# A hybrid decoder step: one Strassen stage for the SSD projections, the gates and the key search, with its weight sums on GpSimd

## The reference

```python
x = x + 0.5 * g1 * swiglu(h, p['w_ffn1_in'], p['w_ffn1_out'])
...
q, k, v, qi, ki, wi, z, xbc, dt_raw, gate_a, gate_s = jnp.split(h @ p['w_in'], split_points(), axis=-1)
...
att = attend(q, k, v, qi, ki, wi)
ssd_y, ssm_new, conv_new = ssd_branch(z, xbc, dt_raw, conv_state, ssm_state, p)
merged = jax.nn.sigmoid(gate_a) * (att @ p['w_attn_out']) + jax.nn.sigmoid(gate_s) * (ssd_y @ p['w_ssd_out'])
x = x + g2 * (merged @ p['w_out'])
...
x = x + 0.5 * g3 * swiglu(h, p['w_ffn2_in'], p['w_ffn2_out'])
```

## Time and profile before

| what | us |
|---|---|
| median of 3 runs (lowest, highest) | 4564.63 (4562.23, 4566.98) |
| the profiled execution | 4567.95 |
| its span | 4566.2 |
| mean granted clock of TensorE | 0.923 |
| the four SSD groups, 1396.31 to 2742.08 | 1345.8 |
| gates and gathers, 2773.7 to 3057.0 | 283.3 |
| attention of the prompt, 3059.8 to 3358.3 | 298.5 |
| second FFN, 3709.0 to 4523.6 | 814.6 |

### The profile page before, as it was taken

One profiled execution on the slowest core, in us unless ns is written; L12 is line 12 of the kernel. 1 busy time (PEld: TensorE's weight loads), 2 busy tenths in 40 slices (PEclk: granted clock), 3 DMA queues, 4 the chain that ended last, 5 costly groups with the idle time before them and its releaser, 6 DMA issues. The chain is left out here.

```text
span 4566.2 us, 47951 instructions
## 1 busy us (share of the span) xinstructions
PE 4077.6 (89%) x17644; PEld 2978.1 (65%) x17644; DVE 2345.6 (51%) x3956; ACT 764.7 (17%) x1512; POOL 292.7 (6%) x325
## 2 busy tenths in 40 slices
PE   6999999969897979979879877988999879999997
PEld 4888888846564646645646644654546558888885
DVE  3444444420038878879789785304453044444444
ACT  2111111121021201201201200015620021111111
POOL 0000000000000200200200200305400000000000
PEclk8999999989968979979979978989998989999999
DMA  4333333241331011011011011220021212222221
GB/s 178 111 138 120 120 122 113 80 195 60 95 56 39 16 55 41 11 57 39 13 55 39 15 53 54 85 93 20 10 70 60 74 55 92 84 81 95 83 86 72
DMA packets 105162, 335.20 MB, mean 73 GB/s; under 512 B 18632, under 2 KB 54736, under 8 KB 86464
## 3 DMA queue, kind: packets, MB, share of 16 engines
q1 hardware_dynamic: 89984, 280.03, 18.2%
q10 hardware_dynamic: 11808, 31.85, 1.9%
q0 software_dynamic: 3200, 21.11, 1.3%
HBM read 289.56 MB, written 43.56 MB: 73 GB/s over the span
## 5 line engine op out<-in xcount | busy, mean ns | idle before, releaser
L737 PE MATMUL banks<-h,arena 128*128 128x344 f32 x1920 | 567.7, 459 | 36.5 <-DMA arena<-in_w_ssd 36.5
L737 PEld LDWEIGHTS banks<-h,arena 128*128 128x128 f32 x1920 | 370.7, 193 | 233.7 <-issue 47.9
L572 ACT ACTIVATE f_u<-f_Y 128x258 f32<-128x258 f32 x408 | 157.7, 387 | 1101.2 <-PE f_Y L510 1101.2
L737 PE MATMUL banks<-y,arena 128*128 128x344 f32 x768 | 239.3, 474 | 38.0 <-DVE y L1938 30.2
L653 DVE TENSOR_TENSOR f_g<-f_u,f_Z 128x258 f32<-128x258 f32 x136 | 57.7, 424 | 390.8 <-PE f_Z L510 390.8
L2122 PE MATMUL gg_ps<-h,gg_w 128*128 128x344 f32 x768 | 234.8, 470 | 9.8 <-DMA gg_w<-in_w_g 9.2
L737 PE MATMUL pja_ps<-h,pja_w 128*128 128x344 f32 x720 | 211.1, 457 | 27.3 <-DMA pja_w<-in_w_att 27.3
L737 PEld LDWEIGHTS banks<-y,arena 128*128 128x128 f32 x768 | 151.7, 199 | 125.6 <-issue 35.7
L2122 PEld LDWEIGHTS gg_ps<-h,gg_w 128*128 128x128 f32 x768 | 151.7, 199 | 90.8 <-DMA gg_w<-in_w_g 10.0
L623 DVE TENSOR_TENSOR f_g<-f_u,f_X 128x258 f32<-128x258 f32 x136 | 57.6, 424 | 292.8 <-PE f_X L510 292.5
L737 PEld LDWEIGHTS pja_ps<-h,pja_w 128*128 128x128 f32 x720 | 138.2, 192 | 100.2 <-issue 29.9
(11 more groups left out here) (354 smaller groups left out, 6814.6 us busy)
## 6 DMA issues: line engine op xcount, KB each, us to landing
raw<-in_w_f1i SPq DMA_DIRECT2D x44, 1024.0 KB, 4.8
raw<-in_w_f2i SPq DMA_DIRECT2D x44, 1024.0 KB, 4.7
f_wa<-in_w_ada SPq DMA_DIRECT2D x14, 2048.0 KB, 9.6
arena<-in_w_ssd SPq DMA_DIRECT2D x40, 512.0 KB, 3.6
raw<-in_w_f1o SPq DMA_DIRECT2D x16, 1024.0 KB, 4.7
raw<-in_w_f2o SPq DMA_DIRECT2D x16, 1024.0 KB, 4.8
n_w<-in_w_ada SPq DMA_DIRECT2D x4, 2048.0 KB, 19.9
scr_kidx<-pja_pages POOLq DMA_DIRECT2D x4, 2048.0 KB, 7.7
```

What stands on the lines that cost most here:

```text
L572: nc.scalar.activation(u[:, i % 2, n], bank[i % 2][:, 0:SUB], ACT.Copy).then_inc(done, 1)
L737: m = nc.tensor.matmul(ps[q][:, c, 0:NC], slots[:, q, k], rhs[:, k, c * NC:(c + 1) * NC], start=k == 0, stop=k == kt - 1)
```

## The change

A new stage, `dense`, stands in place of the four `ssd_project` and of the gates' projection. It runs 28 pairs of output tiles (for each group three convolved ones x, two gate pairs in between, two of z), two halves of columns each, so 56 steps of 7 Strassen products (each 4 matmuls of 128 x 258). `weight_sums` is now told its engine: in `ffn` it is still VectorE, in `dense` GpSimd (`pair_sums`), two pairs ahead. The results go to DRAM: convolved tiles to `scr["xc"]`, activated z and gates to `z`, `gs`, `ga`.

The key search is part of the same stage. The threshold of each row is built bit by bit in 32 steps: `counts` counts on VectorE the scores at or above a candidate (six prompt rows, and the sample scores as two columns of 129 per partition), `vote` adds the sample counts over partitions with one small matmul, and `decide` fixes the bit. Nine later steps mark the chosen keys (`choose`, `choose_samples`).

`index_scores` makes sample scores with four batches side by side in TensorE's column groups (`dot`), a relu and a weighting matmul (`weigh`), and holds four batches of keys at once; they stay in SBUF (`sc2`). `ssd_scan` is written out without a loop and gets its chunks by transfers from DRAM. At the scan's end x and z are loaded for `ssd_post`, which has the skip, gate and norm of `ssd_out` but no projection. `project_and_gather` makes the output projection of all four groups at once, 16 tiles deep, and multiplies it by the gate from DRAM, with a batch's gathers behind each of 8 tiles. `attend` turns up to three chunks ahead and weighs two at a time.

```diff
-def weight_sums(dve, nc, raw, out, made, n):
+def weight_sums(eng, on, raw, out, made, n):
...
+    on.tensor_tensor(s1, a21, a22, ALU.add).then_inc(made, 1)
+    on.tensor_tensor(s3, a11, a21, ALU.subtract).then_inc(made, 1)
+    eng.wait_ge(made, UP + n + 1)
+    on.tensor_tensor(s2, s1, a11, ALU.subtract).then_inc(made, 1)
+    eng.wait_ge(made, UP + n + 3)
+    on.tensor_tensor(s4, a12, s2, ALU.subtract).then_inc(made, 1)
...
-def top_round(dve, nc, rows, m8, found, tick, before):
-
-
-    dve.wait_ge(found, UP + before)
-    dve.sem_inc(tick, 1)
-    for i, s in enumerate(rows):
-        nc.vector.max(m8[0:s.shape[0], i], s).then_inc(found, 1)
-    dve.wait_ge(found, UP + before + len(rows))
-    dve.sem_inc(tick, 1)
-    for i, s in enumerate(rows):
-        nc.vector.match_replace(s, m8[0:s.shape[0], i], s, TAKEN).then_inc(found, 1)
...
+def dense_pairs():
+
+    out = []
+    for g in range(SG):
+        other = [("gs" if g < 2 else "ga", None, (2 * g + n) % 4) for n in range(2)]
+        out += [("x", g, 0), other[0], ("x", g, 1), other[1], ("x", g, 2), ("z", g, 0), ("z", g, 1)]
+    return out
+
...
+            def pair_sums(p):
+                pool.wait_ge(w_in[p % RING], UP + 16 * (p // RING + 1))
+                if p >= SRING:
+                    pool.wait_ge(p3, UP + 2 * (p - SRING) + 2)
+                    pool.wait_ge(p7, UP + 2 * (p - SRING) + 2)
+                weight_sums(pool, nc.gpsimd, raw[:, p % RING].rearrange("p (i k m) -> p i k m", i=4, k=KP), sums[:, p % SRING], made_s, 4 * p)
+
+            for q in range(XB):
+                nc.gpsimd.memset(xb[:, q, :, 0:PAD], 0.0).then_inc(padded, 1)
+            for p in range(SRING):
+                pair_sums(p)
+            for p in range(M):
+                if p in rank:
+                    _, g, j = PAIR[p]
+                    t = g * XT + 2 * j
+                    filled(pool, p)
+                    nc.gpsimd.tensor_copy(raws[:, t:t + 2], xb[:, p % XB, :, PAD + SEQ:PAD + TOK]).then_inc(collected, 1)
+                if p + SRING < M:
+                    pair_sums(p + SRING)
 
...
-            project_tiles(pe, nc, w, ps, h, w_in, mm, read, XT + 4)
+            def product(i, lhs, which, bank, fresh, done):
+                for k in range(KP):
+                    m = nc.tensor.matmul(bank[i % 2][:, 0:SUB], lhs[:, k], column(i, which, k), start=fresh and k == 0,
+                                         stop=k == KP - 1, skip_group_check=not fresh)
+                m.then_inc(done, 1)
+
+            def vote(i):
+                if i < BITS:
+                    pe.wait_ge(counted, UP + (nb + 2) * (i + 1))
+                    if i:
+                        pe.wait_ge(bis, UP + 2 * i)
...
+            for i in range(N + 1):
+                if i < N:
+                    if i % 2 == 0:
+                        pe.wait_ge(w_in[i // 2 % RING], UP + 16 * (i // 2 // RING + 1))
+                    if i >= 2:
+                        pe.wait_ge(yread, UP + i - 1)
+                    product(i, left(i, 0), "11", Y, True, p1)
+                    if i >= 2:
+                        pe.wait_ge(xread, UP + i - 1)
+                    product(i, left(i, 1), "21", X, True, p2)
+                if i >= 1:
+                    pe.wait_ge(u3, UP + i)
+                    product(i - 1, left(i - 1, 3), "t4", Y, False, p4)
+                if i < N:
+                    pe.wait_ge(made_h, UP + 4 * (i % 2 + 1) if i < 2 else UP + 8)
+                    pe.wait_ge(u1, UP + i + 1)
+                    pe.wait_ge(made_s, UP + 4 * (i // 2) + 4)
+                    product(i, total(i)[:, 1], "t2", Y, False, p6)
+                if i >= 1:
+                    pe.wait_ge(zhalf, UP + i)
+                    product(i - 1, total(i - 1)[:, 3], "22", Z, False, p3)
+                if i < N:
+                    if i >= 2:
+                        pe.wait_ge(zread, UP + i - 1)
+                    product(i, total(i)[:, 0], "t1", Z, True, p5)
+                    pe.wait_ge(u2, UP + i + 1)
+                    product(i, total(i)[:, 2], "t3", Y, False, p7)
+                vote(i)
...
+            def counts(j, ns):
+                for n in ns:
+                    scratch, done = (pre, eq)[n % 2], (nb + 2) * j + n
+                    if done >= 2:
+                        dve.wait_ge(counted, UP + done - 1)
+                    src = rows[n] if n < nb else sc2[:, n - nb]
+                    nc.vector.tensor_scalar(scratch[:, 0:src.shape[1]], src, thr(n), None, ALU.is_ge, ALU.add,
+                                            accum_out=count[:, n:n + 1]).then_inc(counted, 1)
+
+            def decide(j):
+                dve.wait_ge(counted, UP + (nb + 2) * (j + 1))
+                dve.wait_ge(ballot, UP + j + 1)
+                nc.vector.tensor_scalar(ok[:, 0:nb], count[:, 0:nb], float(TOPK), -1.0, ALU.is_ge, ALU.mult).then_inc(bis, 1)
+                nc.vector.tensor_scalar(ok[:, nb:], pC[:, 0:2], float(TOPK), -1.0, ALU.is_ge, ALU.mult).then_inc(bis, 1)
+                dve.wait_ge(bis, UP + 2 * j + 2)
+                ch.link(nc.vector.tensor_tensor(ok[:], ok[:], bits[:, j], ALU.bitwise_and))
+                ch.link(nc.vector.tensor_tensor(cur[:], cur[:], ok[:], ALU.bitwise_xor))
+                ch.link(nc.vector.tensor_tensor(cand[:], cur[:], bits[:, j + 1], ALU.bitwise_xor))
...
+            for i in range(N + 1):
+                if i >= 1:
+                    half(i - 1)
+                if 1 <= i <= BITS:
+                    decide(i - 1)
+                if i < BITS:
+                    counts(i, range(3))
+                if i < N:
+                    first(i)
+                if i < BITS:
+                    counts(i, range(3, nb + 2))
+                if i >= 1:
+                    rest(i - 1)
+                if i >= 2 and i // 2 - 1 in rank:
+                    convolve(i // 2 - 1, i % 2)
...
-            def stage(c, s):
-                if not isinstance(c, int):
-                    act.wait_ge(yoff, UP + c - 1)
-                nc.scalar.activation(st[:, s], xc[:, :, bass.ds(c * P, P)], ACT.Copy).then_inc(staged, 1)
-
...
+            for c in range(TB):
+                if c >= 2:
+                    sp.wait_ge(yoff, UP + c - 1)
+                sp.dma_start(st[:, c % 2], xc[:, :, c * P:(c + 1) * P]).then_inc(staged[c % 2], 16)
+            if first is not None:
+                first(sp)
...
+            for t in range(KT):
+                pe.wait_ge(w_in[t % 2], UP + 16 * (t // 2 + 1))
                 for c in range(NCH):
-                    if not (isinstance(i, int) and i == 0 and q == 0):
-                        pe.wait_ge(gread, UP + NCH * (2 * i + q - 1) + c + 1)
-                    for k in range(KT):
-                        m = nc.tensor.matmul(ps[:, c, 0:NC], w[:, q, k], h[:, k, c * NC:(c + 1) * NC],
-                                             start=k == 0, stop=k == KT - 1)
-                    m.then_inc(gmm, 1)
-
...
-                turn(u, 0)
-                turn(u, 1)
-                for c in range(b + 1):
-                    weigh(u, c)
-                    if c == half(u) and u + AHEAD < N:
+                for c in range(min(RING, b + 2)):
+                    turn(u, c)
+                ahead, scored = min(RING, b + 2), u + AHEAD >= N
+                for c in range(0, b + 1, 2):
+                    for e in range(c, min(c + 2, b + 1)):
+                        weigh(u, e)
+                    if c + 1 >= half(u) and not scored:
                         scores(u + AHEAD, 1)
-                    if c + 2 <= b + 1:
-                        turn(u, c + 2)
-                if half(u) > b and u + AHEAD < N:
+                        scored = True
+                    while ahead < min(c + 2 + RING, b + 2):
+                        turn(u, ahead)
+                        ahead += 1
+                if not scored:
                     scores(u + AHEAD, 1)
 
```

More of the change, by code:

```diff
@@ L904, in _, with prompt @@
-            sp.wait_ge(stored, UP + 32)
+                    sp.dma_start(kx[half * ID:(half + 1) * ID, j], src).then_inc(k_in[j], 16)
         @block.tensor
         def _(pe):
-            pe.wait_ge(small, UP + 80)
+            def prompt(n):
+                b, t = PAIRED[n]
+                W = (b + 1) * P
+                for u in range(2):
+                    if n:
+                        pe.wait_ge(relu, UP + 2 * (n - 1) + u + 1)
+                    for c in range(0, W, 512):
+                        e = min(c + 512, W)
+                        m = nc.tensor.matmul(ps[:, u, c:e], pj[64 * u:64 * u + ID, QI0 + t, b * P:(b + 1) * P],
+                                             pj[64 * u:64 * u + ID, KI0, c:e], start=True, stop=True)
+                    m.then_inc(mm[u], 1)
@@ L909, in _ @@
+            pe.wait_ge(small, UP + 16 * 7)
             pe.wait_ge(prodd, UP + 1)
-            for u in range(4):
-                m = nc.tensor.matmul(pN[:, 2 * u:2 * u + 2], prod[:, u], hot[:], start=True, stop=True)
```

(50 more changed lines are left out.)

839 lines of the change are left out of this document (469 added, 370 removed).

## The result

The changed kernel takes 4430.62 us in the median of four runs (4429.05 to 4436.24), 0.9708 of the kernel before (95% interval 0.9691 to 0.9725): about 134 us less, where 86 were forecast. The forecast was 4478 us, so the kernel is 47 us faster than that.

What follows compares the result with a forecast made beforehand. TensorE was taken as the bound, VectorE right behind in the SSD groups. Groups -66, gates and gathers -12, attention -12, index scores +4 sum to -86: 4482 us, as a median 4478; range 4415 to 4535, the forecast's own 4440 to 4515.

Steps and rivals of the forecast that it cites:

- the groups: Dense stage plus four times scan, sample and post: 1282 us against 1345.8 + 2.5 before, so -66.
- Dense, products: Dense stage: 3136 Strassen matmul instructions at the second FFN's price take 691 us; the votes add 11.
- Dense, waits of the votes: Dense stage's key search: votes wait for VectorE about 3 us in each of seven convolution pairs, 21 (0 to 35).
- GpSimd's sums in time: Dense stage: GpSimd's four weight sums take 4.2 to 4.9 us a pair, with 18 us available.
- Scan, sample, post: Rest of each SSD group: 70.5, 35 and 28.7 us, with 1.1 us of stall for each of six scan chunks.
- Gates and gathers: Projection and gathers stage: 274 us against 283.3, both before a 3 us barrier; -12 (0 to -17).
- Attention: Prompt attention: turning up to three ahead wins a little under half of 26.4 us idle, -12 (+5 to -25).
- Index scores: Index scores stage: some 20 us of matmul saved, but waits for keys of 10 and 15; +4 (-10 to +18).
- all is hidden: Rival: cheap counts, interleaved sums, chunks in time, attention -25; total 4406 us, chance 0.14.
- The clock: Rival: dense stage's stops at votes lower the clock; at 0.88 +93, no change. Chance 0.08, of which 0.05 slower.
- the change's last part gives nothing back: Rival, here denied: VectorE bounds the dense stage and, with late scan chunks, total is 4539 us; chance 0.18.
- The sums did not come too late: Rival, here denied: GpSimd's dense-stage sums come too late, needing over 18 us instead of 4.9; no chance given.

Runs made afterwards that it cites:

- four-buffer run: Changed kernel with the scan's chunks in four buffers in place of two, each asked for two turns earlier: 4405.32 us, ratio 0.9641 to the kernel before.

## Why the prediction was right, and where it was 47 us off

- **The total** is inside the range, but below the forecast's own 4440 to 4515: the groups came 27 us lower, gates and gathers 14, the index scores 15, and the attention 7 higher.
- **What bounds it** held for the dense stage (TensorE busy 697.9 of 720.3 us) and the projection (237.6 of 260.4). It does not hold for the small stages of a group: VectorE is the busier in the sample step (24.6 against 20.6) and in the post stage (21.3 against 9.0), as it already was in the output stage before (73.5 against 69.5), where the prediction read TensorE as the bound.
- **Dense, products:** right. 697.9 busy with the votes, against 691 + 11.
- **Dense, waits of the votes:** the step "it waits 31.4 - 25.2 - 3.6, about 3 us. Seven convolution pairs lie in the search: 7 x 3 = 21" was mis-sized; 1.7 measured. The mechanism was right and its terms were each a little high: VectorE's plain step is 7.6 us busy, 8.3 with its own short waits for TensorE, and not 8.9 (consecutive counts start closer than they last), and the lock cost a pair 72 x (1730 - 1286)/12 = 2.7 us in the long operations and 0.8 in the next decision, not 4.4. Set into the same sum, 2 x (8.3 + 4.6) + 3.5 = 29.3, less two steps of 12.4 and the 4.1 left of the third, is 0.4 us a pair; 1.7/7 = 0.24 was measured. It lies on an edge: the experiments with doubled sums (about 3 us more in one decision) and doubled counts (some 6 more in each step) pay 56 and 128.
- **GpSimd's sums in time:** right; one wait of 1.8 us. Their price was mis-sized: the four means add up to 6.7 us for a pair, not 4.2 to 4.9, and 18 us were enough even so. By the Trainium skill, "SBUF — State Buffer", section "Who interferes with whom", a `tensor_scalar` that also writes out its accumulator stays off the port shared with GpSimd, and an operation with two SBUF inputs contends with a GpSimd instruction that reads SBUF; the trace agrees, 1276 ns beside GpSimd and 1274 without for a count of 1024, 1730 and 1285 for the convolution.
- **Scan, sample, post:** 70.8, 34.6 and 27.4 against 70.5, 35 and 28.7: right, and the four-buffer run shows the scan's reason. (58.0 + 6 x 1.1 + 2.8 is 67.4 and not the 67.7 of the forecast, and in the dense stage the lower bound of the counts is 4482 x 744/1024 = 3.3 us before short ones' start, not 3.6; nothing hangs on either.)
- **Gates and gathers:** "the one-hot matmuls keep 266.0 - 234.8 = 31" failed. They take 14. Before (L2142) and after (L2373):

```profile
L2142 PE MATMUL gg_pE<-gg_vals,gg_hots 128*128 x512 | 31.5, 171 | 0.3
```

```profile
L2373 PE MATMUL gg_pE<-gg_vals,gg_hots 128*128 128x3 f16 x512 | 14.0, 164 | 0.0
```

  Before, the products of two batches stood in a loop, and the trace has a register operation on TensorE's queue for every two of them:

```profile
L2142 PEldq FUSED_REGOPS  x256: 46/55/60, 2828.6 to 2912.4; - x128
```

  Such operations follow each other 0.133 us apart. The first 26 of 128 products come 0.025 us apart, the others about 0.067, in step with them, and all 128 take some 8 us. They did not wait for VectorE: in the second turn of the loop the one-hots had ended at 2852.47 us, and the products began at 2857.23. Nor was it the clock: it was 1.00 up to 2861 us, when they already came 0.067 us apart. Written out without a loop there is no register operation, all 64 products of a batch come 0.025 us apart and take 1.75. That the register operations are the cause is read from this; no run put them back. The last gathers and the barrier were dearer than 11 + 3, 17 us from the end of the last products to the next stage, and the first loads took 7.8 in place of 5.
- **Attention:** the step "It has 298.5 - 272.1 = 26.4 us to win; I take half less a little" failed. The new order wins nothing of that idle time: TensorE is idle 31.7 us of the stage now, and its waits for other engines add up to 23.6 us, where they were 18.4 before and are 19.0 in the run with the old order. What fell is TensorE's busy time, which is modelled: 261.8 us in place of 272.1, and 269.0 in the run with the old order. Together that is -4.6, of which the order is 2 to 6; why the busy time fell stays open.
- **Index scores:** the sign was wrong. The step "the second four are asked for only after the first four's last dot: 15 more", with the 10 ahead of it, was mis-sized: 14.3 in five waits, 5.5 for the first four batches and 8.8 for the second, since a landed batch's products run while the next one comes, and 8 us of other work stand between the first four's last product and the second four's first. The new products cost 21.7 + 10.9 against 47.8, 15 less. What I had not priced at all is the clock, 0.68 in place of 0.59: the prompt's products of 512 and 384 columns take 42.7 + 12.5 us where they took 53.0 + 14.6, 12 less (the first row is of before):

```profile
L932 PE MATMUL sel_ps<-pj 64*128 64x512 f32 x96 | 53.0, 1002 | 6.6 <-ACT sel_r L952 6.6
```

```profile
L925 PE MATMUL sel_ps<-pj 64*128 64x512 f32 x96 | 42.7, 817 | 7.7 <-ACT sel_r L985 7.7
```

  14 - 15 - 12 is -13, near the -11.3 measured. In other profiles of the same code the stage is up to 7 us shorter, so this term is known to no better than that.

The forecast's rivals: of "all is hidden" the dense part came, scan and attention did not. The clock stayed at 0.99 in the dense stage. VectorE does not bound that stage, so the change's last part gives nothing back; the runs with sums on VectorE show that it gains nothing that can be told either. The sums did not come too late.

## What to carry to other kernels

Where one engine's late work delays another only past a margin, write the margin down in the trace's own numbers (3.9 us here), and forecast both sides of it: a sum of small terms each a little high made a wait of 21 us out of 1.7. Moving the sums to an idle engine gained nothing that could be told while the relieved engine was hardly awaited, and what such a move costs through the lock depended on which instructions it fell on, not only on its length. A transfer in place of a copy needs buffers for its landing time: two more were worth some 25 us.

## What the runs showed of the hardware

- Beside GpSimd a VectorE operation of 6 or 8 columns takes as long as a GpSimd instruction has left: 0.90 to 1.19 us in place of 0.17. GpSimd's sums take 1.27 us alone and 2.24 between VectorE's long operations, as each waits for the other in turn. One of each then takes about 2.2 us, less than the 1.29 + 1.27 of the two alone, so they still overlap by some 0.35 us.
- Counts that accumulate are not delayed, though GpSimd works through them (1276 and 1274 ns); they start before the one ahead has ended (0.61 us long, 0.54 apart).
- The index stage's granted clock differs between runs of the same code, and the stage with it: over the same stretch 0.67 and 0.68 in the two profiles of 121 us, 0.71 in two of 117 to 118, 0.75 and 0.76 in those of 114 to 115. The waits for keys don't explain it, 14.3 us in one of the longest and 18.2 in one of the shortest. What decides it stays open.
- Small matmuls with a register operation for every two of them come 0.067 us apart, without any 0.025.
